# Starting on two DMA queues and norming in pairs: the first stretch of a fused two-block kernel

## The reference

```python
c_act = jax.nn.silu(c)
mod = c_act @ ada_w[layer] + ada_b[layer]          # 6 x 1024 numbers: shift, scale, gate, twice
shift_m, scale_m, gate_m, shift_f, scale_f, gate_f = jnp.split(mod, 6)
h = rmsnorm(x, norm_mix_g[layer]) * (1.0 + scale_m) + shift_m
proj = h @ w_in                                    # q, k, v, gate: 4 x 1024 columns
a_in, b_in = proj[..., 4096:4104], proj[..., 4104:4112]    # two gates of 8 heads each
# second block, later: keys and values of a memory of 256 tokens
kv = rmsnorm(mem, c_mem_norm[i]) @ c_wkv[i]
```

## Time and profile before

| | us |
|---|---|
| median of 3 runs (2260.78 to 2264.84) | 2261.49 |
| the profiled execution | 2262.04 |
| its span, first to last instruction | 2260.3 |
| PE busy in the span | 2165.2 (96%) |
| DVE / ACT / POOL busy | 1178.9 / 581.7 / 1211.3 |
| first matmul on h (gate weights, chunk 0) | 69.98 |
| the sum of gdn slab 0 is copied | 81.64 |

### The profile page before, as it was taken

One profiled execution on the slowest core, in us unless ns is written; L12 is line 12 of the kernel. 1 busy time (PEld: TensorE's weight loads), 2 busy tenths in 40 slices (PEclk: granted clock), 3 DMA queues, 4 the chain that ended last, 5 costly groups with the idle time before them and its releaser, 6 DMA issues.

```text
span 2260.3 us, 29283 instructions
## 1 busy us (share of the span) xinstructions
PE 2165.2 (96%) x11996; PEld 1727.9 (76%) x11996; DVE 1178.9 (52%) x1634; ACT 581.7 (26%) x1054; POOL 1211.3 (54%) x688
## 2 busy tenths in 40 slices
PE   5999999889999999998999999999999999999998
PEld 4777777777888887676788888777767778877886
DVE  3666666657638275454531322467765365346333
ACT  4433433213202022342320201422332230012113
POOL 4532233346868776433566666654445266656663
PEclk9999999999999999999999999999999999999999
DMA  9422222226556463211333333322223133333331
GB/s 303 143 67 85 86 83 85 85 66 213 178 168 205 140 198 106 75 45 38 118 94 96 100 94 100 96 75 75 66 62 116 38 112 94 99 87 93 103 103 66
DMA packets 366016, 240.40 MB, mean 106 GB/s; under 512 B 11350, under 2 KB 350524, under 8 KB 365756
## 3 DMA queue, kind: packets, MB, share of 16 engines
q1 hardware_dynamic: 364268, 234.60, 34.4%
q10 hardware_dynamic: 1616, 3.93, 0.5%
HBM read 234.31 MB, written 4.19 MB: 106 GB/s over the span
## 4 chain that ended last, share of the span: by engine, by line
PE 87%; DVE 6%; ACT 2%; issue 2%; POOL 1%; DMA 1%; SPq 0%; ACTq 0%; DVEq 0%; POOLq 0%
PE bank L578 16%; PE bank L580 16%; PE bank L579 16%; PE bank L597 6%; PE bank L599 5%; PE bank L598 5%; PE mid L846 2%; PE mid L1297 1%; PE bank L614 1%; DMA stage<-in_c_wkv 1%; PE bank L616 1%; PE bank L615 1%; PE bank L815 1%; PE mid L622 1%; PE bank L817 1%
## 5 line engine op out<-in xcount | busy, mean ns | idle before, releaser
L532 POOL TENSOR_SCALAR wH<-stage 128x1024 fp32r<-128x1024 f32 (+1 forms) x340 | 380.4, 1119 | 993.0 <-PE bank L599 375.6
L534 POOL TENSOR_TENSOR wL<-stage,wH 128x1024 fp32r<-128x1024 f32 (+1 forms) x340 | 830.3, 2442 | 28.4
L578 PE MATMUL bank<-hH,wH 128*128 128x512 f32 x944 | 368.7, 391 | 0.7 <-DVE A L2004 0.3
L580 PE MATMUL bank<-hH,wL 128*128 128x512 f32 x944 | 367.4, 389 | 0.0
L579 PE MATMUL bank<-hL,wH 128*128 128x512 f32 x944 | 367.3, 389 | 0.0
L578 PE MATMUL bank<-RA,wH 128*128 128x512 f32 (+1 forms) x836 | 304.3, 364 | 4.6 <-DVE RA L2018 1.8
L579 PE MATMUL bank<-RA,wH 128*128 128x512 f32 (+1 forms) x836 | 301.4, 361 | 0.0
L580 PE MATMUL bank<-RA,wL 128*128 128x512 f32 (+1 forms) x836 | 301.1, 360 | 0.0
L597 PE MATMUL bank<-hH,wH 128*128 128x512 f32 x544 | 238.7, 439 | 0.3 <-DVE A L2004 0.3
L599 PE MATMUL bank<-hH,wL 128*128 128x512 f32 x544 | 213.7, 393 | 0.0
L598 PE MATMUL bank<-hL,wH 128*128 128x512 f32 x544 | 213.0, 391 | 0.0
(11 more groups left out here) (382 smaller groups left out, 3171.4 us busy)
## 6 DMA issues: line engine op xcount, KB each, us to landing
WIDE<-in_ada_t SPq DMA_DIRECT2D x48, 1024.0 KB, 6.1
stage<-in_ffn_w_gate SPq DMA_DIRECT2D x44, 512.0 KB, 3.9
stage<-in_ffn_w_up SPq DMA_DIRECT2D x44, 512.0 KB, 3.9
stage<-in_c_wkv SPq DMA_DIRECT2D x32, 512.0 KB, 4.0
stage<-in_gdn_w_in SPq DMA_DIRECT2D x32, 512.0 KB, 4.1
stage<-in_ffn_w_down SPq DMA_DIRECT2D x32, 512.0 KB, 4.0
stage<-in_o_w_in SPq DMA_DIRECT2D x32, 512.0 KB, 4.0
stage<-in_e_w_in SPq DMA_DIRECT2D x26, 512.0 KB, 3.9
```

Of the source, the lines that this page charges most:

```text
L532: pool.tensor_scalar(high[:, 0:n], raw[:, 0:n], 1.0, 0.0, ALU.mult, ALU.add).then_inc(w_high, 1)
L534: pool.tensor_tensor(low[:, 0:n], raw[:, 0:n], high[:, 0:n].bitcast(F32), ALU.subtract).then_inc(w_split, 1)
L578: pe.matmul(bank[:, 0:n], h[:, k, c], xh[:, k, :], start=first and k == 0, stop=False)
L580: mm = pe.matmul(bank[:, 0:n], l[:, k, c], xh[:, k, :], start=False, stop=last and k == kc - 1)
```

## The change

- **ScalarE's queue.** ScalarE now issues, before anything else, the loads of c, x and the first two modulation groups, and after the memory rows the third. SP issues only 256 columns of the tables first; the rest of the tables comes after kv slabs 0 and 1.
- **Groups.** The order of the first eight groups becomes 0, 4, 1, 5, 2, 6, 3, 7 (`ADA_ORDER`), so shift and scale of one pair of chunks come together. They have three buffers instead of two; the third lies in `A[:, 12:16]`. The text calls them first to eighth in this new order.
- **The norm by pairs.** DVE sums the first four groups, norms the pairs of chunks 0-1 and 2-3 (`first_norm`), sums the fifth and sixth, norms pair 4-5, sums the seventh and eighth, norms pair 6-7.
- **The early work.** The memory is turned into four banks instead of two, DVE's part of it comes before the first group sum, the Ln/Exp table is loaded before the memory rows, and kv slabs, turns of x and squares are interleaved one step earlier each.
- **The gate weights.** High and low half of the 16 gate columns lie side by side in one tile, so two matmuls a chunk do what three did; their sum is added afterwards by two small DVE instructions.

```diff
+ADA_ORDER = (0, 4, 1, 5, 2, 6, 3, 7)
+        adaw.append(A[:, 12:16].rearrange("p (r a) t -> p r (a t)", r=ADA_ROWS))
+        def ada_use(n):
+            return (n % 3, n // 3 + 1) if n < ADA_HEAD else (n % 2, (n - ADA_HEAD) // 2 + 4)
+        mem_banks = ((B3, B7, B4, SS), (B3, B7, B3, B7))
...
             def load_ada(n):
-                if n >= 2:
-                    sp.wait_ge(ada_summed, n - 1)
+                slot = ada_use(n)[0]
+                if n >= 3:
+                    sp.wait_ge(ada_summed, n - 2 if n < ADA_HEAD else n - 1)
...
-            sp.dma_start(cbc[:], a["c"].broadcast_to((P, D))).then_inc(c_in, 16)
-            load_ada(0)
-            load_ada(1)
-            load_ada(2)
-            sp.dma_start(A[:, 0:8].rearrange("p (t a) c -> p t (a c)", t=TT),
-                         a["x"][0].rearrange("(t p) d -> p t d", p=P)).then_inc(x_in, 16)
...
+            act.dma_start(cbc[:], a["c"].broadcast_to((P, D))).then_inc(c_in, 16)
+            act.dma_start(A[:, 0:8].rearrange("p (t a) c -> p t (a c)", t=TT),
+                          a["x"][0].rearrange("(t p) d -> p t d", p=P)).then_inc(x_in, 16)
+            for n in range(2):
+                rows = a["ada_t"][0].rearrange("(n r p) k -> n p r k", p=P, r=ADA_ROWS)
+                act.dma_start(adaw[n], rows[ADA_ORDER[n]]).then_inc(ada_loaded[n], 16)
             act.wait_ge(c_in, 16)
             own(act.activation(cbc[:], cbc[:], ACT.Silu))
             own.settle()
             act.activation(c_bank, cbc[:], ACT.Copy).then_inc(m["c"], 1)
+            act.preload_act_table_set(LN_EXP)
             memory_rows(0)
+            act.dma_start(adaw[2], rows[ADA_ORDER[2]]).then_inc(ada_loaded[2], 16)
...
# PE
-                pe.matmul(B3[:], h, hH[:, k, :], start=k == 0, stop=False)
-                pe.matmul(B3[:], h, hL[:, k, :], start=False, stop=False)
-                mm = pe.matmul(B3[:], l, hH[:, k, :], start=False, stop=k == KD - 1)
+                both = RA[:, 0, 32 * k:32 * k + P]
+                pe.matmul(B3[:], both, hH[:, k, :], start=k == 0, stop=False)
+                mm = pe.matmul(B3[:], both, hL[:, k, :], start=False, stop=k == KD - 1)
...
# ScalarE, after the copies of kv slabs 0 to 3, the turns and the squares of x
+            inv_sqrt(ss_done, SS0[1], SS, SS[:], 1.0 / D, load=False).then_inc(rstd_ready, 1)
+            early_copies((4, 5))
+            first_high(range(2))
+            early_copies((6,))
+            first_high(range(2, 4))
+            early_copies((7,))
+            early_spill(1)
+            first_high(range(4, KD))
...
# DVE
-            ada_sum(0)
             for n in range(4):
                 memory_low(0, n)
-            for n in range(1, ADA_HEAD):
-                ada_sum(n)
-            gain_of(0, col["mix0"], 8)
-            norm("mix0", gainA[:, 0], modT[:, 0:8])
+            for n in range(4):
+                ada_sum(n)
+            dve.wait_ge(x_ready, KD)
+            dve.wait_ge(rstd_ready, 1)
+            for pair in range(2):
+                first_norm(pair)
+            for pair in range(2, 4):
+                for n in range(2 * pair, 2 * pair + 2):
+                    ada_sum(n)
+                first_norm(pair)
```

More of the change, by code:

```diff
@@ L228, in build @@
         gate_row = RA[0:64, 14:16]
-        ab_raw, ab_high, ab_low = A[:, 14, 0:384], RA[:, 0, 0:384], RA[:, 1, 0:384]
+        ab_raw, ab_pads = tb[:, 0, 0:128].rearrange("p (k c) -> p k c", c=16), RA[:, 0, 256:384]
+        ab_high, ab_low = (RA[:, 0, 0:256].rearrange("p (k c) -> p k c", c=32)[:, :, 16 * n:16 * n + 16] for n in range(2))
         early_kv = A[:, 8:12].rearrange("p a (b t) -> p (a b) t", t=MEM)
@@ L278, in build @@
         taken = [sem(f"taken{n}") for n in range(2)]
-        ada_loaded = [sem(f"ada_loaded{n}") for n in range(2)]
+        ada_loaded = [sem(f"ada_loaded{n}") for n in range(3)]
         ada_summed, c_in = sem("ada_summed"), sem("c_in")
+        tab_in = sem("tab_in")
         small_in, x_in, vec_in, par_in, wide_in, mem_in = (
@@ L534, in split @@
                 pool.tensor_tensor(low[:, 0:n], raw[:, 0:n], high[:, 0:n].bitcast(F32), ALU.subtract).then_inc(w_split, 1)
-            for j in range(2):
-                pool.memset(ab_raw[:, 192 * j + 64:192 * j + 192], 0.0).then_inc(pool_own, 1)
+            pool.memset(ab_pads.bitcast(F32), 0.0).then_inc(pool_own, 1)
             def split_gates():
-                pool.wait_ge(pool_own, 2)
                 pool.wait_ge(g["ab_in"], 32)
@@ L687, in memory @@
                     pe.wait_ge(m["mem"], r + 1)
-                if n >= 2:
+                if r and n >= 2:
                     pe.wait_ge(x_memt, r * 8 + 2 * n - 2)
@@ L1451, in memory_rows @@
                     own.settle()
-                own(inv_sqrt(act_own, own.now(), mss[:, 2:4], mss[:, 0:2], 1.0 / D))
+                own(inv_sqrt(act_own, own.now(), mss[:, 2:4], mss[:, 0:2], 1.0 / D, load=r == 1))
                 own.settle()
@@ L1521, in kv_copies, with first_high @@
                         act.activation(to, (B3, B7)[j][:, 0:MEM], ACT.Copy).then_inc(kv_copied, 1)
-            early_copies(range(2))
+            def first_high(ks):
+                for k in ks:
+                    act.wait_ge(t_ready, k + 1)
+                    act.activation(hH[:, k, :], (B4, B7)[k % 2][:], ACT.Identity, bias=modT[:, k:k + 1]).then_inc(hh_ready, 1)
+            early_copies((0,))
             x_copies(range(4))
+            early_copies((1,))
+            x_copies(range(4, KD))
             early_copies((2,))
-            x_copies(range(4, KD))
+            squares_of_x(range(4))
             early_copies((3,))
             early_spill(0)
-            squares_of_x(range(4))
-            early_copies((4,))
             squares_of_x(range(4, KD))
-            early_copies((5,))
-            rstd_of(RUN_OF["mix0"], SS)
-            early_copies((6, 7))
+            inv_sqrt(ss_done, SS0[1], SS, SS[:], 1.0 / D, load=False).then_inc(rstd_ready, 1)
[4 more added lines that the diff above has]
+            early_copies((7,))
             early_spill(1)
-            norm("mix0", modT[:, 0:8], load=False)
+            first_high(range(4, KD))
             q, k_, v, gs0, E, dec, gs1, LT, kdec, XT, ktok, wT, Pm, vn = (A[:, n] for n in range(14))
@@ L2257, in _ @@
             own(dve.reciprocal(tok[:, 1], tok[:, 1]))
[L2259 to L2260 removed]
+            dve.wait_ge(g["eb"], 2)
+            own(dve.scalar_tensor_tensor(out=tmp8[:, 1], in0=tmp8[:, 1], scalar=0.0, in1=tmp8[:, 2], op0=ALU.max, op1=ALU.add))
             own.settle()
```

92 lines of the change are left out of this document (56 added, 36 removed).

## The result

| | before | after |
|---|---|---|
| median of all runs, us | 2263.12 (6 runs, 2260.78 to 2265.25) | 2270.06 (6 runs, 2268.97 to 2271.88) |
| the profiled execution / its span | 2262.04 / 2260.3 | 2268.97 / 2266.8 |
| kv slab 0 on PE (S) | 25.57 | 26.17 |
| the mark: gdn slab 0 copied | 81.64 | 89.07 |

The change makes the kernel 0.32% slower: the ratio is 1.0032, 95% interval 1.0022 to 1.0042. The mark moved by 7.4 us, the profiled execution by 6.9, the medians by 6.9. So the loss lies ahead of the mark, as forecast, and it is close to the 6.2 us of the sum.

The account below looks back on a forecast made before the run. PE, holding 87% of the chain of waits, bounds the kernel. Kv slab 0's start 22.6 + 54.0 + 9.0 + 2.2 = 87.8 against 81.6, 6.2 us later: median 2267.7, range 2263.5 to 2272.0.

Parts of the forecast that it names:

- the sum: Time until gdn slab 0 is done: 22.6 + 54.0 + 9.0 + 2.2 = 87.8 against 81.6, 6.2 us later.
- The memory: Memory load at the kernel's start: lands at 10.8 instead of 12.3, bounds 12.3 and 9.3.
- kv slab 0: First kv slab: split between 16.9 (even bytes) and 23.5 (packet turns); middle taken, PE starts it at 22.6.
- From S on: PE and norm after kv slab 0 starts: kv 7 done at S+40.3, first `hH` S+35.0, fifth sum S+42.8.
- The eighth group and gdn slab 0: SP's queue: both loads issued only after the fifth sum, S+42.8; slab lands 7.7 later, split at S+54.0.
- PE idle: PE before gdn slab 0: stands still 13.7 us, then 9.0 for 38 matmuls plus 2.2 for a lower clock.
- The gates': Two added DVE instructions before the gates' sums: about 0.2 us each, at most 0.4, nothing on PE's path.
- The milder one: Rival: memory lands at 9.3, kv slab 0 starts at 20.2; +2.7 us, 2264.2; chance 0.25.
- The faster one: Rival: eighth group's wait does not reach PE, which goes straight on from kv 7; -9.2 us, 2252.3; chance 0.07.
- The slower rival: kv slab 2 comes 3 us late behind the conv weights' tiny packets, delaying everything behind; 2270.7; chance 0.09.

Follow-up runs that it names:

- e3: Changed kernel with x and the first two groups issued on ScalarE's queue only after silu(c) and the table load: 2269.0 us, ratio 1.0028.
- e12: Changed kernel with c, x and the first two groups loaded on SP's queue, order kept, only the third group on ScalarE's: 2269.6 us, ratio 1.0031.
- e6: Changed kernel with x loaded by four DMAs of 256 columns, packets of 1 KB instead of 4 KB: 2268.5 us, ratio 1.0021.
- e2: Changed kernel with DVE summing all eight groups before the first norm pair: 2257.8 us, ratio 0.9973.
- e4: Changed kernel with all eight sums before the first norm pair and x and two groups issued after silu(c): 2257.7 us, ratio 0.9976.
- e7: e4 with SP's small loads (gate weights, rest of tables, columns, parameters, conv weights) behind kv slabs 2 and 3: 2253.9 us, ratio 0.9959.
- e8: e7 with the eighth group's load ahead of kv slab 7's in SP's queue: 2255.8 us, ratio 0.9970.
- e9: e7 with parameters and conv weights moved between the eighth group and gdn slab 0 in SP's queue: 2257.7 us, ratio 0.9970.
- e10: e2 with parameters and conv weights moved behind the eighth group in SP's queue: 2256.4 us, ratio 0.9968.

## Why the prediction was right, and where its steps were off

The mechanism of the loss was right: the fifth sum behind two norm pairs, the eighth group's load behind that sum, gdn slab 0 behind that load, PE idle. The time, 2270.1 against 2267.7, lies in the range. One step ahead of it was wrong. Step by step:

- **The memory** is the step that failed. It was to land at 10.8, in bounds of 12.3 and 9.3 that excluded a loss; it landed at 15.5. I had reasoned that the bytes until then stay at some 2.4 MB and that a second queue can only fill a hole. In the stretch 0:15.5 of the changed kernel (packets, MB and share of each queue) nearly 5 MB moved:

```profile
q10 hardware_dynamic: 902, 3.55, 60.5%
q1 hardware_dynamic: 879, 1.41, 27.1%
```

  ScalarE's c, x and first group took their turns with 4 KB packets against vectors of 512 B, and then every other packet against the memory. I had weighed turns by packets for kv slab 0, but left them out for the memory. e3 (9.8), e12 (9.5) and e6 (11.4) each took that away in another way, and each time it landed sooner.
- **kv slab 0.** I took the middle between two ways of sharing, even bytes and turns of packets. The counts of e6 and of the changed kernel show turns of packets. The slab was split only at 24.8, but the late memory covered it: PE waited for DVE's `memory_low` at S. From the memory's landing to the first turn it took 5.2 us and from there to S 5.4, as in the sum (5.2 and 5.7). S = 26.2 instead of 22.6: I had it 3.6 too early, and it lies outside my bounds of 20.2 to 25.0.
- **From S on** the intervals held. kv slab 7 was copied at S+39.8 (predicted 40.3), the first `hH` stood at S+34.3 (35.0), the fifth sum ended at S+41.9 (42.8).
- **The eighth group and gdn slab 0.** Issued within 0.5 us of that sum's end. The slab landed 6.5 us after its issue, where I took 7.7 with a bound of 6.6.
- **PE idle** 12.1 us instead of 13.7, then 10.5 for the slab where I had 9.0 + 2.2. The first seven matmuls were slow, at 0.43 instead of 0.23, which makes 1.4 us.
- So S was 3.6 too early and the terms behind it 2.3 too long in sum: 89.07 against 87.8 at the mark. The error in the memory was larger than the result shows; two errors of opposite sign met. That the number came so close is in part luck.
- **The gates'** two DVE instructions took 0.22 each (92.02 and 92.27 in DVE's timeline), as said.
- **The rivals.** The milder one is refuted, since S rose. The faster one is what e2 builds: once the fifth sum doesn't hold the slab, PE goes on with short stops of 1.5 us in all, and its mark of 77.84 is S+51.2, where that rival had S+49.8. The slower rival, kv slab 2 late, did not show in the changed kernel, because S was late itself; in e3, e4 and e12 it did, with 3.0 to 4.5 us.

What stays open: how much of e7's lead of some 2 to 4 us over e2, e4, e8, e9 and e10 is its own. Their intervals overlap, their marks lie within 1.7 us of one another, and five to eleven runs of each don't part them. All six are faster than the kernel before.

## What to carry to other kernels

Put work that waits for nothing (here sums of loaded groups) into the time in which an engine waits for something else, and look what its end releases: a sum that frees a buffer also frees everything that stands behind that buffer's load in an in-order queue. A second DMA queue added no bandwidth where the first was full (409 GB/s with one in the stretch 9:12, 402 with two), and the two took turns by packets; so loads with large rows should not run beside loads that are needed first, above all not beside those with small rows. When one start is made earlier, the next load in line must be made earlier with it, or the gain is given back there (three kernels here waited 3.0 to 4.5 us at kv slab 2). And a load that is moved back in a queue is not gone: it meets the load behind it (e9).
